# Column sums of the modulation vectors: the data as moving operand in four column tiles of TensorE, and a 32x32 transposition on VectorE

## The reference

```python
mod = jax.nn.silu(c) @ p['w_mod'][l] + p['b_mod'][l]
sh1, sc1, g1, sh2, sc2, g2, sh3, sc3, g3 = jnp.split(mod, N_MOD, axis=-1)
h = _rmsnorm(x, ng[0]) * (1.0 + sc1) + sh1
x = x + g1 * 0.5 * _swiglu(h, w_gate, w_up, w_down)      # first feed-forward half-step
h = _rmsnorm(x, ng[1]) * (1.0 + sc2) + sh2               # then attention and a recurrent unit
...
h = _rmsnorm(x, ng[2]) * (1.0 + sc3) + sh3               # then the second feed-forward half-step
```

## Time and profile before

| | |
|---|---|
| median of 3 runs | 2306.4 us (2306.05 to 2315.53) |
| span of the profiled execution | 2307.2 us |
| TensorE matmul busy | 2221.6 us (96%) |
| VectorE busy | 1541.2 us (67%) |
| ScalarE busy | 819.0 us (35%) |
| mean granted TensorE clock | 0.989 |

### The profile page before, as it was taken

The page is one execution under the profiler, slowest core; times in us unless marked ns, Lnnn a source line. Parts: engine busy times, 40 slices in busy tenths (PEclk is TensorE's granted clock), DMA queues, the critical chain, the costliest instruction groups (busy, mean ns, idle before and its releaser), DMA issues.

```text
span 2307.2 us, 33872 instructions
## 1 busy us (share of the span) xinstructions
PE 2221.6 (96%) x13080; PEld 2117.2 (92%) x13080; DVE 1541.2 (67%) x2586; ACT 819.0 (35%) x1462; POOL 27.1 (1%) x34
## 2 busy tenths in 40 slices
PE   5989999999999999999989999999999999999997
PEld 3989999999999998778967779999999999999997
DVE  5977676777878775675558884586545456746556
ACT  5622222334111143654236663344323233412122
POOL 0000000000000000000010030000000000000000
PEclk9999999999999999999999999999999999999999
DMA  7433233244524303011000011222122223441212
GB/s 285 131 103 131 103 121 112 94 134 140 208 81 158 124 19 147 1 37 59 32 23 22 24 40 38 73 91 79 66 77 69 73 70 107 139 141 49 97 55 83
DMA packets 82288, 209.52 MB, mean 91 GB/s; under 512 B 9984, under 2 KB 36480, under 8 KB 82176
## 3 DMA queue, kind: packets, MB, share of 16 engines
q1 hardware_dynamic: 82176, 207.99, 26.6%
HBM read 172.04 MB, written 35.92 MB: 90 GB/s over the span
## 4 chain that ended last, share of the span: by engine, by line
PE 90%; DVE 6%; ACT 2%; issue 1%; DMA 1%; DVEq 0%; ACTq 0%
PE ps L691 18%; PE ps L693 17%; PE ps L692 17%; PE ps L783 9%; PE ps L784 9%; PE ps L785 9%; PE ps L1011 4%; PE ps L1040 2%; PE ps L950 2%; PE ps L1026 1%; DVE sb_nmx L2221 1%; PE ps L732 1%; DVE sb_hL L1719 1%; DVE sb_tmp L1728 1%; DVE sb_last_raw L1670 0%
## 5 line engine op out<-in xcount | busy, mean ns | idle before, releaser
L691 PE MATMUL ps<-sb_hH,sb_wH 128*128 128x384 f32 x1664 | 562.6, 338 | 6.3 <-DVE sb_hL L1719 2.9
L692 PE MATMUL ps<-sb_hL,sb_wH 128*128 128x384 f32 x1664 | 557.8, 335 | 0.0
L693 PE MATMUL ps<-sb_hH,sb_wL 128*128 128x384 f32 x1664 | 557.6, 335 | 0.0
L691 PEld LDWEIGHTS ps<-sb_hH,sb_wH 128*128 128x128 f32 x1664 | 313.7, 189 | 10.1 <-DVE sb_hL L1719 4.1
L692 PEld LDWEIGHTS ps<-sb_hL,sb_wH 128*128 128x128 f32 x1664 | 313.7, 188 | 1.1
L693 PEld LDWEIGHTS ps<-sb_hH,sb_wL 128*128 128x128 f32 x1664 | 313.6, 188 | 0.0
L2023 DVE SCALAR_TENSOR_TENSOR sb_x<-ps,sb_mod,sb_x 128x384 f32<-128x384 f32 (+2 forms) x384 | 186.4, 514 | 181.4 <-PE ps L693 176.6
L783 PE MATMUL ps<-sb_hH,sb_wH 128*128 128x384 f32 x704 | 235.4, 334 | 1.7 <-issue 0.9
L784 PE MATMUL ps<-sb_hL,sb_wH 128*128 128x384 f32 x704 | 235.2, 334 | 0.0
L785 PE MATMUL ps<-sb_hH,sb_wL 128*128 128x384 f32 x704 | 235.2, 334 | 0.0
L1330 ACT ACTIVATE sb_wH<-sb_raw 128x512 fp32r<-128x512 f32 (+1 forms) x96 | 57.0, 596 | 379.2 <-PE ps L693 371.2
(11 more groups left out here) (242 smaller groups left out, 3643.8 us busy)
## 6 DMA issues: line engine op xcount, KB each, us to landing
sb_raw<-in_w_gate SPq DMA_DIRECT2D x56, 512.0 KB, 3.5
sb_raw<-in_w_up SPq DMA_DIRECT2D x56, 512.0 KB, 3.5
sb_raw<-in_w_mod SPq DMA_DIRECT2D x56, 512.0 KB, 3.6
hidden<-sb_tmp SPq DMA_DIRECT2D x132, 192.0 KB, 2.3
sb_hid_raw<-hidden SPq DMA_DIRECT2D x40, 576.0 KB, 6.3
sb_raw<-in_w_dn SPq DMA_DIRECT2D x80, 256.0 KB, 2.7
sb_stage<-in_w_mod SPq DMA_DIRECT2D x4, 2048.0 KB, 15.0
sb_raw<-in_w_in SPq DMA_DIRECT2D x16, 512.0 KB, 3.8
```

Source lines behind the costliest of these rows:

```text
L691: pe.matmul(o, wH, xH, start=begin, stop=False)
L692: pe.matmul(o, wH, xL, start=False, stop=False)
L693: return pe.matmul(o, wL, xH, start=False, stop=end)
```

## The change

- `mod_collect`: `ones[:, 0:32]` becomes the weights, and `rq` and `modp` become the moving operand. Each of the two takes four products, one for each column tile of the array. Column tile r streams the 128 columns whose number, divided by 32, has the remainder r when divided by 4, and writes their sums to partitions 32r to 32r+31, all 32 alike. `quadrants` issues the four.
- `mod_collected`: a transposition of the 32x32 squares of the 128x256 result on VectorE into `modp` turns the sums so that they lie along the partitions. Then the same scaling and bias as before, from SBUF. There are two new waits of VectorE on its own instructions: one between the two, and one behind the second.
- `mod_products`: the same split. Eight times, once for each 128 rows of depth, four products of 128 columns, all of depth accumulated in PSUM: 32 products for a block where there were eight. `mod_evac`, `mod_total` and `sel` are gone. `mod_add` transposes 128x128 and adds the bias.
- The order on TensorE in the opening is now block 0, `spread`, blocks 1, 2, 3; on ScalarE the four copies are gone.

```diff
+            def quadrants(bank, at, weights, src, begin, end):
+                for r in range(4):
+                    m = pe.matmul(by_tile(ps[32 * r:32 * r + 32, bank, at:at + P]), weights, by_quadrant(src)[:, r],
+                                  start=begin, stop=end, tile_position=(0, 32 * r))
+                return m
             def mod_collect(b, n):
                 pe.wait_ge(mod_acc, n * 16)
                 pe.wait_ge(mod_done, b)
-                for k in range(4):
-                    for cond, src in ((0, rq), (1, modp)):
-                        m = pe.matmul(ps[:, 7, 2 * k + cond:2 * k + cond + 1], src[:, k * P:(k + 1) * P], ones[:, 0:1],
-                                      start=True, stop=True)
-                m.then_inc(mod_sum, 1)
+                quadrants(7, 0, ones[:, 0:32], rq[:], True, True)
+                quadrants(7, P, ones[:, 0:32], modp[:], True, True).then_inc(mod_sum, 1)
             def mod_products(n):
...
-                mod_partial(stage[MOD_FIRST[n]], mod_bank(n))
+                src = stage[MOD_FIRST[n]]
+                for k in range(KT):
+                    m = quadrants(mod_bank(n), 0, cs[:, k, :], src[:, k // 2, k % 2 * 512:k % 2 * 512 + 512], k == 0, k == KT - 1)
+                m.then_inc(mod_sum, 1)
             mod_products(0)
-            mod_finish(0)
             spread(0, 0)
-            mod_products(1)
-            mod_finish(1)
-            mod_products(2)
-            mod_products(3)
-            mod_finish(2)
-            mod_finish(3)
+            for n in range(1, PRE):
+                mod_products(n)
...
             root_of(0, 0)
-            mod_evac(0)
             root_copy(0, 0)
-            mod_evac(1)
...
-            h_hi(0, 0, range(3))
-            mod_evac(2)
-            h_hi(0, 0, (3,))
-            mod_evac(3)
+            h_hi(0, 0, range(4))
...
                 dve.wait_ge(mod_sum, n + 1)
-                dve.tensor_tensor(mod[:, at], ps[:, mod_bank(n), 0:8].rearrange("p (n c) -> p n c", c=2), bmod[:, at],
+                turned = modp[:, n * P:(n + 1) * P]
+                link(dve.transpose(turned, ps[:, mod_bank(n), 0:P]))
+                dve.tensor_tensor(mod[:, at], turned.rearrange("p (n i) -> p n i", i=32)[:, :, 0:2], bmod[:, at],
                                   ALU.add).then_inc(mod_done, 1)
             def mod_collected(b):
...
-                dve.scalar_tensor_tensor(mod[:, at], ps[:, 7, 0:8].rearrange("p (n c) -> p n c", c=2), float(D), bmod[:, at],
-                                         ALU.mult, ALU.add).then_inc(mod_done, 1)
+                turned = modp[:, 0:2 * P]
+                dve.transpose(turned, ps[:, 7, 0:2 * P]).then_inc(mod_turn, 1)
+                dve.wait_ge(mod_turn, b - (PRE - 1))
+                totals = turned.rearrange("p (c n i) -> p n c i", c=2, i=32)[:, :, :, 0]
+                dve.scalar_tensor_tensor(mod[:, at], totals, float(D), bmod[:, at], ALU.mult, ALU.add).then_inc(mod_done, 1)
+                dve.wait_ge(mod_done, b + 1)
```

More of the change, by code:

```diff
@@ L160, in build @@
             cin = sb("cin", [P, KT, 2], F32, s)
-            sel = sb("sel", [P, 2], F32, s)
             bmod = sb("bmod", [P, 9 * KT, 2], F32, s)
@@ L210, in build @@
         c_ready = sem("c_ready")
-        mod_prod = sem("mod_prod")
-        mod_copy = sem("mod_copy")
         mod_sum = sem("mod_sum")
+        mod_turn = sem("mod_turn")
         mod_done = sem("mod_done")
@@ L418, in build @@
                   (convb[:], "convb"), (gbias[:], "gbias"), (glam[:, 0], "glam"), (h0[:], "h0"),
-                  (subg[:], "subg"), (sel[:], "sel"))
+                  (subg[:], "subg"))
         N_SMALL = 16 * len(SMALLS)
@@ L429, in stats_bank, with by_quadrant, by_tile @@
             return 7 if z % 2 else (4 if z == 0 else 7, 0, 1)[c]
+        def by_quadrant(src):
+            return src.rearrange("p (n r j) -> p r n j", n=4, r=4)
+        def by_tile(w):
+            return w.rearrange("p (n j) -> p n j", n=4)
         def mod_bank(n):
@@ L740, in mod_products @@
                     pe.wait_ge(mod_done, n - 1)
-                mod_partial(stage[MOD_FIRST[n]], mod_bank(n))
-            def mod_finish(n):
-                pe.wait_ge(mod_copy, n + 1)
-                mod_total(mod_bank(n))
+                src = stage[MOD_FIRST[n]]
+                for k in range(KT):
+                    m = quadrants(mod_bank(n), 0, cs[:, k, :], src[:, k // 2, k % 2 * 512:k % 2 * 512 + 512], k == 0, k == KT - 1)
+                m.then_inc(mod_sum, 1)
             pe.wait_ge(cons, 1)
@@ L1172, in load_root @@
                 act.activation(unused[:], eps[:, 0:1], ACT.Sqrt).then_inc(table, 1)
[L1174 to L1178, removed]
             def one_cast(o, full, used=None, slot=None, other=False):
@@ L2383 @@
     cos, sin = rope_tables()
-    sel = np.zeros((P, 2), np.float32)
-    for q in range(4):
-        sel[32 * q, 0] = sel[32 * q + 1, 1] = 1.0
     w3 = np.asarray(w_in)[0]
@@ L2420 @@
         "sin": sin,
-        "sel": sel,
         "ident": np.eye(P, dtype=np.float32),
```

## The result

| | before | changed |
|---|---|---|
| median | 2310.24 us, 4 runs (2306.05 to 2315.53) | 2293.22 us, 4 runs (2290.62 to 2297.25) |
| span of the profiled execution | 2307.2 us | 2288.8 us |
| TensorE matmul busy | 2221.6 us | 2201.2 us |
| VectorE busy | 1541.2 us | 1549.0 us |

The changed kernel takes 0.9924 of the time, interval 0.9899 to 0.9948, which is 17.6 us less (12 to 23); the two medians alone differ by 17.0 us. The forecast was 16.8 us less and 2289.6 us. It started from 2306.4, the median of the first three runs; with the fourth the kernel before is at 2310.24 us, so the saving is the number to compare. The time of a run is 1.8 us above the span of the same execution here (2290.62 and 2288.8 us).

What follows compares the result with a forecast made beforehand. TensorE, busy 96% of the span, bounds the kernel; in the opening, a VectorE and ScalarE chain. Collects 14.0 plus opening 2.8 make 16.8 us, off the median 2306.4 gives 2289.6 us; range 2283 to 2299.

Steps and rivals of the forecast that it cites:

- The collects: 14 `mod_collect` calls on TensorE: each falls from 1.78 to 0.78 us, saving 1.00 us, 14.0 us in all.
- the switch of `stats`: Leaving and regaining TensorE's full array, contained in the 0.51 us of `stats`' eight rows, on which the 0.78 us call builds.
- That the loads do not hide: Rival, column tiles on TensorE: every round pays its weight load, collects save only 8.4 us, total 2297 us; chance 0.12.
- VectorE's price: VectorE behind each collect: the added transposition with its two waits costs 0.5 us per block.
- the cover: VectorE's idle time before L1851: about 3.5 of 4.54 us stay and hide the added work, otherwise 7 us return.
- The opening: First four blocks: VectorE reaches L1755 at about 35.1, 2.8 us earlier; bounds none to 3.5 us.
- now it starts at about 19.8, and the copy at 20.75: Opening: `spread` directly after block 0 starts at 19.8 instead of 21.31, ScalarE's copy at 20.75 instead of 22.23.
- the chain: Opening, VectorE and ScalarE: L1719 at 25.0 instead of 28.48, then L1755 at about 35.1.
- the rival of the fourth block: Rival: a transfer or the fourth block ends last, so the opening gives at most 1 us; 2292 us; chance 0.15.
- The slower rival: Collects on TensorE: four tiles read one after the other, 3.5 us a call, 2335 us or above; chance 0.04.
- the "more than forecast" one: Rival: switches overlap with the longer calls, collects save 17 us and more, 2286 us; chance 0.05.

Runs made afterwards that it cites:

- the doubled call: Changed kernel with the eight products of each collect issued twice, one after the other; 2296.51 us (one run).
- the change again: The changed kernel, unaltered, run once more in the series with its parts, against the kernel before; 2297.43 us, ratio 0.9932.
- thirteen transpositions: Changed kernel with each collected block transposed thirteen times on VectorE instead of once; 2325.25 us.
- the collects alone: Kernel before with only the 14 collects changed (`mod_collect`, `mod_collected`), the opening as before; 2298.54 us, ratio 0.9937.
- the forty products: Changed kernel with 40 unused products of ones by ones on TensorE ahead of `stats`; 2291.55 us (one run).

## Why the prediction was right, and where it was off

**The collects** were forecast to save 1.00 us each, and saved 1.04 (loop 1.04, and likewise behind it: 31.98 instead of 33.02 us between two collects of the down projection). The distance was forecast at 1.13 us and is 1.12; the rest of the 0.04 is in the products behind, to the eighth of which 2.17 us pass instead of 3.21. The terms behind it hold one by one: 0.85 ns a column measured against 0.84 from the earlier trace rows, so that the switch of `stats` could be carried over. That the loads do not hide was the rival that goes with a rule of the Trainium skill ("TensorE: Matmul & The Clock Gate", Part 3, Packing small matmuls): weight loads overlap with products in flight only when the row group differs. The runs do not agree with it. All four tiles here share their row group, and the loads run beside the products at 128 columns as they had at 512. With a load of 0.11 us unhidden in each round the doubled call would have cost 0.87 us more, and it cost 0.43.

**VectorE's price** was mis-sized: 0.5 us forecast, 0.88 measured. The transposition itself, 0.44 us, lay in its range. What was short is the rest. In the loop 154.72 - 153.77 = 0.95 us pass from the transposition to L1810, and before it was 0.07 us from L1684 to L1827. In this stretch, beside 0.44 and 0.17 of work, stand 0.20 us of waiting for its own result and 0.14 us behind the scaling, where the second wait is.

It did no harm, since the cover was forecast at 3.5 us and the experiments with more transpositions show it to be real. I had looked for its end at the wrong place, though: what is thin is not the place behind a collect, but `mod_part` ahead of the ninth, with half a microsecond.

**The opening** was forecast at 2.8 us and gave 2.26 to the first feed-forward product, 1.57 to the first collect. The step that was off is "now it starts at about 19.8, and the copy at 20.75": it lets `spread` run at its former 0.89 us. In the changed trace `spread` took 1.65 us from 19.54 on, and the copy came at 21.23, 0.48 us later than forecast. That is the 0.5 us by which `h_hi` came at 24.68 and not at 24.15.

It is not the new place right behind block 0 that makes `spread` slow. In the same order it took 0.91 us in three other traces. TensorE's timeline of the change again:

```profile
15.87 3.22 PE L720 MATMUL ps<-sb_stage,sb_cs 128*32 128x128 f32 x64 [0.18 <-ACT sb_cs L1385]
19.02 0.91 PE L714 MATMUL ps<-sb_tmp,sb_ones 128*128 128x384 f32 x2
```

In the others it took 1.14, 1.44 and 1.65 us. What differs is when the slow pace of the start ends: between 18.5 and 21.2 us in the seven openings of the new form, at 19.5 before. The forecast had only one execution to go by and took its moment along, so this half microsecond is a matter of chance. Where the moment was nearly the same (thirteen transpositions, 19.8 us) the gain to the first product was 2.6 us.

Behind that the chain held as worked out: from L1702 to L1738 it took 10.11 us, as forecast (35.1 - 25.0). The fourth block came 0.7 us later than before (TensorE takes it up at 31.06), and did not end last. In the change again it did: it ran at the slow pace from 31.40 to 35.04, VectorE waited 1.58 us for it, and the first product came at 36.80 in spite of the fast `spread`. There the rival of the fourth block is what bounds the opening. Until the first collect the lead changes with the clock: it is 2.26 us at the product that stood at 45 us before, 0.68 at 50, behind a stretch of the changed kernel at the lower clock from 45.0 to 48.4 in which products are 0.32 us apart and not 0.17, and 1.57 again at 80; such stretches fall here and there in the first 50 us of all traces.

**What made the total come out closer than its terms:** the collects gave 0.6 us more than forecast (14.6 for 14.0) and the opening 1.2 less (1.6 for 2.8), which offset each other in part, by luck. Together they make 16.1 us, and 2.2 us of the two spans come from less time at the lower clock far behind. The medians, 17.6 us (12 to 23) and 15.7 (11 to 20), cannot tell these apart. The slower rival, tiles one after another, is refuted by the distance of 1.12 us; the "more than forecast" one by the switch of 0.34 us that is still there.

## What to carry to other kernels

Where TensorE adds up over the partitions between other products, count both ways: one column behind a 128x128 load costs the load, a stream through the whole array costs its columns, and only four column tiles at a time beat both. Look for a row of the same mode amid the same neighbours, since it has the price of the switch in it. Don't take the duration of a row near the start from one execution: its pace changes at a moment that differs from execution to execution, so price it at both paces. Work without use in a gap moved the slow stretch here, in the one run that tried it, and did not remove it.

## What was not expected of the hardware

- The granted clock that a window shows for the start is not measured there. In the changed trace block 0 takes 3.64 us for the work that block 1 does in 1.95, and the window over both says 1.00. With the collects alone `spread` and block 1 ran at half pace from 22.1 to 27.3 us, and the window says 1.00 too:

```profile
14.00:24.00 10.00, 7.65 (x138) 5.38 (x138) 4.08 (x14) 6.33 (x10) 0.00 (x0) 1.00 1.03 412
```

```profile
20.00:33.00 13.00, 11.55 (x66) 4.71 (x66) 3.16 (x11) 5.76 (x11) 0.00 (x0) 1.00 1.02 406
```

  The clock record of a trace, from which the windows are worked out, begins only at 21.1 us in the changed kernel, at 19.5 before, at 27.8 with the collects alone and at 7.8 with the forty products, and a stretch without a record is counted as full. In each trace the rows are slow up to that moment and fast behind it. They look like rows at the lower level (0.50, 1.2 GHz): the fourth block takes 3.46 us where the record says 0.54 on average. That the clock stood at this level before its first record is therefore likely, but no row says it. Until the record begins, only the durations of the rows tell the pace.

- A transposition on VectorE from PSUM took 0.32 us for 128 float32 columns and 0.44 us for 256, less than a copy of 384 (0.55 us).
- A wait of VectorE on its own last result cost 0.20 us in the loop, where the awaited value comes from a register. Behind the loop, where the value is fixed, the same two instructions follow each other within 0.03 us (478.94 + 0.44 to 479.41), as in the opening (34.25 + 0.32 to 34.60). That the register makes the difference was not tested by itself.
- The same old opening came to the first feed-forward product at 38.63 in one execution and at 41.87 in another. The slow pace of the start lasted until 19.5 us in the one and until 27.8 in the other, though TensorE had begun at 15.3 in both and done the same work up to 19.5. What decides this stays open.
